# Recurrent branch's matmul units by token instead of by feature, its convolution spread over two units

## The reference

```python
h = rmsnorm(x, norm_mix_pre[l])
proj = h @ w_in[l]
xr, yr, q, k, v, g_rnn, g_attn = jnp.split(proj, IN_OFFSETS, axis=-1)
xr = causal_depthwise_conv(xr, conv_w[l], conv_b[l])   # y[s] = b + sum over k of xr[s-3+k] * w[k]
xr = rg_lru(xr, positions, ...)                        # gates by 256x256 blocks, then a scan over tokens
y_rnn = xr * jax.nn.gelu(yr)
q = rope(...); k = rope(...)
y_att = sliding_window_sink_attention(q, k, v, attn_sinks[l])
mix = sigmoid(g_rnn) * (y_rnn @ w_rnn_proj[l]) + sigmoid(g_attn) * (y_att @ w_attn_proj[l])
```

## Time and profile before

| | us |
|---|---|
| time, median of 3 runs | 2236.02 (2235.87 to 2236.43) |
| time of the profiled execution | 2235.79 |
| its span in the profile | 2234.1 |
| PE busy | 2226.4 (100%) |
| DVE busy | 1576.0 (71%) |
| ACT busy | 1223.8 (55%) |
| GpSimd busy | 274.0 (12%) |

### The profile page before, as it was taken

One profiled execution on the slowest core, in us unless ns is written; L12 is line 12 of the kernel. 1 busy time (PEld: TensorE's weight loads), 2 busy tenths in 40 slices (PEclk: granted clock), 3 DMA queues, 4 the chain that ended last, 5 costly groups with the idle time before them and its releaser, 6 DMA issues.

```text
span 2234.1 us, 32770 instructions
## 1 busy us (share of the span) xinstructions
PE 2226.4 (100%) x11630; PEld 1873.3 (84%) x11630; DVE 1576.0 (71%) x2081; ACT 1223.8 (55%) x1925; POOL 274.0 (12%) x317
## 2 busy tenths in 40 slices
PE   9999999999999999999999999999999999999999
PEld 7888999888888888888888888889977788778887
DVE  7666657665664778757857856966999967766774
ACT  6666677544444456555555656556444446554443
POOL 1232220000000102111212121120000001100000
PEclk9999999999999999999999999999999999999999
DMA  7555554666666866666666666665666665555665
GB/s 245 156 166 150 152 179 146 194 192 194 194 189 198 255 197 200 214 206 191 219 205 193 216 209 203 193 220 184 181 187 203 195 180 175 162 161 178 198 200 167
DMA packets 215349, 427.09 MB, mean 191 GB/s; under 512 B 14096, under 2 KB 14384, under 8 KB 214960
## 3 DMA queue, kind: packets, MB, share of 16 engines
q1 hardware_dynamic: 206960, 398.57, 57.4%
q0 software_dynamic: 8048, 26.62, 3.8%
q10 hardware_dynamic: 208, 0.07, 0.0%
HBM read 414.71 MB, written 10.49 MB: 190 GB/s over the span
## 4 chain that ended last, share of the span: by engine, by line
PE 92%; DVE 4%; ACT 3%; issue 1%; DMA 0%; POOL 0%; SPq 0%; ACTq 0%; POOLq 0%; DVEq 0%
PE acc L2054 25%; PE acc L2056 25%; PE acc L2055 25%; PE acc L2046 4%; PE acc L2048 3%; PE acc L2049 3%; DVE w_lo L1217 1%; PE sides L2274 1%; PE tps L2284 1%; PE sides L2147 1%; ACT w_hi L677 1%; PE tps L2165 1%; PE acc L1997 1%; PE tps L2158 0%; DVE stg L1241 0%
## 5 line engine op out<-in xcount | busy, mean ns | idle before, releaser
L1217 DVE TENSOR_TENSOR w_lo<-raw,w_hi 128x1024 fp32r<-128x1024 f32 x752 | 928.4, 1244 | 581.6 <-ACT w_hi L677 575.9
L677 ACT ACTIVATE w_hi<-raw 128x1024 fp32r<-128x1024 f32 x752 | 789.7, 1058 | 727.6 <-PE acc L2056 594.2
L2054 PE MATMUL acc<-w_hi,h_hi 128*128 128x512 f32 x1424 | 563.0, 395 | 0.3 <-DVE w_lo L1217 0.2
L2056 PE MATMUL acc<-w_hi,h_lo 128*128 128x512 f32 x1424 | 554.8, 390 | 0.0
L2055 PE MATMUL acc<-w_lo,h_hi 128*128 128x512 f32 x1424 | 554.5, 389 | 0.0
L2054 PEld LDWEIGHTS acc<-w_hi,h_hi 128*128 128x128 f32 x1424 | 267.3, 188 | 66.1 <-issue 11.4
L2056 PEld LDWEIGHTS acc<-w_hi,h_lo 128*128 128x128 f32 x1424 | 267.3, 188 | 56.7
L2055 PEld LDWEIGHTS acc<-w_lo,h_hi 128*128 128x128 f32 x1424 | 267.6, 188 | 52.8
L2054 PE MATMUL acc<-w_hi,slab_dg_r 128*128 128x512 f32 x756 | 294.2, 389 | 0.0
L2055 PE MATMUL acc<-w_lo,slab_dg_r 128*128 128x512 f32 x756 | 294.1, 389 | 0.0
L2056 PE MATMUL acc<-w_hi,slab_dg_r 128*128 128x512 f32 x756 | 294.1, 389 | 0.0
(11 more groups left out here) (407 smaller groups left out, 2356.8 us busy)
## 6 DMA issues: line engine op xcount, KB each, us to landing
raw<-in_w_in_dram SPq DMA_DIRECT2D x328, 512.0 KB, 4.0
raw<-in_w_mlp_up_dram SPq DMA_DIRECT2D x128, 512.0 KB, 4.2
raw<-in_w_mlp_down_dram SPq DMA_DIRECT2D x128, 512.0 KB, 4.2
raw<-in_w_out_dram SPq DMA_DIRECT2D x64, 512.0 KB, 4.6
raw<-in_w_rnn_proj_dram SPq DMA_DIRECT2D x32, 512.0 KB, 3.9
raw<-in_w_attn_proj_dram SPq DMA_DIRECT2D x32, 512.0 KB, 4.1
trig_scratch<-tmp POOLq DMA_DIRECT2D x32, 256.0 KB, 4.8
raw<-in_w_proj_ssm_dram SPq DMA_DIRECT2D x16, 512.0 KB, 3.8
```

The source lines that it names most:

```text
L677: nc.scalar.activation(w_hi[:, j % RING], raw[:, j % RING], ACT.Copy).then_inc(hi_ready, 1)
L1217: V.tensor_tensor(w_lo[:, j % RING], raw[:, j % RING], w_hi[:, j % RING].bitcast(F32), ALU.subtract)\
L2054: T.matmul(o, hi[:, k, c], wh, start=first, stop=False)
L2056: ins = T.matmul(o, lo[:, k, c], wh, start=False, stop=last)
```

## The change

The four xr units are made by token. When one is done, ACT copies the result to SBUF with `rstd` as a scale per partition (`xr_stage`, two instructions), and DVE turns it in 16 transposes of 32-row blocks (`xr_turn`, eight pieces of two) into `xr_c`; `xr_out` is gone. For c = 0 to 2 five pieces lie in steps 1, 1, 3, 3, 5 of the second unit and three in steps 2, 2, 4 of the next xr unit; for c = 3 all lie in yr0, in steps 1, 1, 3, 3, 4, 4, 5, 5. ACT's taps come one a step, for c = 0 to 2 in steps 5 and 7 of the next xr unit and in steps 2 and 4 of the unit after that; for c = 3 in steps 6, 6, 7, 7 of yr0. GpSimd adds the taps of c - 1 between the norms of c, and those of c = 3 last; `load_rg(0)` goes to after the sums of c = 2. `xr_c` and the staging get buffers of their own per c. The loops over c of ACT and DVE are written out.

```diff
@@ GpSimd
                     for c in range(NH):
                         normalise(None, c, 0)
                         normalise(None, c, 1)
+                        if c:
+                            conv_sum(c - 1, 2)
                         normalise(None, c, 2)
+                        if c:
+                            conv_sum(c - 1, 1)
                         normalise(None, c, 3)
-                        for k in (2, 1, 0):
-                            conv_sum(c, k)
-                        if c == 0:
-                            load_rg(0)
+                        if c:
+                            conv_sum(c - 1, 0)
+                    pool.wait_ge(tap_ready, 4 * (NH - 1))
+                    load_rg(0)
+                    for k in (2, 1, 0):
+                        conv_sum(NH - 1, k)
                     pool.wait_ge(conv_ready, NH + 1)
                     load_rg(1)
@@ places
-        TAPS_AT = [8, 10, 13, 13]
+        XR_TURN_AT = [1, 1, 3, 3, 5, S + 2, S + 2, S + 4]
+        TAPS_AT = [S + 5, S + 7, 2 * S + 2, 2 * S + 4]
+        LAST_TURN_AT = [1, 1, 3, 3, 4, 4, 5, 5]
+        LAST_TAPS_AT = [6, 6, 7, 7]
@@ ACT
+                def xr_stage():
+
+                    unit_over(None, 0, (U_QX + 1 + 2 * c) * S)
+                    if c == NH - 1:
+                        act.wait_ge(stg_ready, T_QX + c + 1)
+                    for t in range(TT):
+                        ins = nc.scalar.activation(xr_stage_of(c)[:, t, :], tok(acc[0])[:, t, :], ACT.Copy, scale=rstd[:, t:t + 1])
+                    ins.then_inc(acc_free[0], 1)
                 def conv_taps(k):
 
                     if k == 3:
-                        act.wait_ge(acc_free[0], lin(i, 1, c + 2))
-                        act.wait_ge(conv_ready, lin(i, 1, c + 1))
+                        act.wait_ge(xr_turned, c + 1)
+                        act.wait_ge(conv_ready, c + 1)
@@ ACT, gates
-                    act.wait_ge(conv_ready, NH + 1)
+                    act.wait_ge(conv_ready, NH)
@@ DVE
+            def turn_two(n, to, of):
+
+                for q in (2 * n, 2 * n + 1):
+                    a, b = divmod(q, 4)
+                    src = of[32 * a:32 * a + 32, :, :].rearrange("p t (m q i) -> p t m q i", q=4, i=32)[:, :, :, b, :]
+                    dst = to[32 * b:32 * b + 32, :, :].rearrange("p m (t q i) -> p t m q i", t=TT, q=4)[:, :, :, a, :]
+                    ins = V.transpose(dst, src)
+                return ins
+                def xr_turn(n):
+                    if n == 0:
+                        dve.wait_ge(acc_free[0], c + 2)
+                        if c == 2:
+                            dve.wait_ge(tap_ready, 4)
+                    ins = turn_two(n, xr_c[c], xr_stage_of(c))
+                    if n == 7:
+                        ins.then_inc(xr_turned, 1)
-            def xr_out(i, c):
-                unit_over(i, 2 * S, (U_QX + 1 + 2 * c) * S)
-                rows_ = row[:, :].unsqueeze(1).broadcast_to([P, QPC, SEQ])
-                dve.wait_ge(row_copied, 1)
-                dve.wait_ge(conv_ready, lin(i, 1, c + 1))
-                V.tensor_tensor(xr_c, feat(acc[0]), rows_, ALU.mult).then_inc(acc_free[0], 1)
@@ TensorE
-                unit(None, 0, u * S, 0, u, h_hi, h_lo, by_feature=True, hooks=beside_xr)
+                unit(None, 0, u * S, 0, u, h_hi, h_lo, hooks=beside_xr)
-            unit(None, 0, (U_QX + 2 * NH - 1) * S, 0, U_QX + 2 * NH - 1, h_hi, h_lo, by_feature=True, hooks=beside_xr)
+            unit(None, 0, (U_QX + 2 * NH - 1) * S, 0, U_QX + 2 * NH - 1, h_hi, h_lo, hooks=beside_xr)
```

More of the change, by code:

```diff
@@ L179, in griffin_block_then_ssm_block @@
         part_hi, part_lo = sem("part_hi"), sem("part_lo")
+        xr_turned = sem("xr_turned")
         side_landed = sem("side_landed")
@@ L358, in griffin_block_then_ssm_block @@
         xc4 = stg[:, :, :].rearrange("p t (k c) -> p (t k) c", c=SEQ)
-        xr_c = i4
+        xr_c = [slab_g[:, 0:4, :], i4, slab_g[:, 0:4, :], tmp2[:, :, :].rearrange("p t (k c) -> p (t k) c", c=SEQ)]
         yr_c = [k_t[:, :, :], xc4]
@@ L636, in griffin_block_then_ssm_block, with xr_stage_of @@
         TURN_P_AT = [13, 18, 23, 28]
-        TAPS_AT = [8, 10, 13, 13]
+        XR_TURN_AT = [1, 1, 3, 3, 5, S + 2, S + 2, S + 4]
+        TAPS_AT = [S + 5, S + 7, 2 * S + 2, 2 * S + 4]
+        LAST_TURN_AT = [1, 1, 3, 3, 4, 4, 5, 5]
+        LAST_TAPS_AT = [6, 6, 7, 7]
+        def xr_stage_of(c):
+            if c == NH - 1:
+                return tmp
+            return slab_d[:, (c + 1) * QPC:(c + 2) * QPC, :].rearrange("p k c -> p (k c)").rearrange("p (t n) -> p t n", t=TT)
         Y_ATT_AT = [(k + 3) // 2 for k in TURN_P_AT]
@@ L820, in conv_taps @@
                             ins = nc.scalar.activation(slab_d[:, span(i, QPC, QPC * c + m), :].rearrange("p o c -> p (o c)"),
-                                                       xr_c[:, m, :], ACT.Identity, scale=w, bias=b)
+                                                       xr_c[c][:, m, :], ACT.Identity, scale=w, bias=b)
                         else:
-                            ins = nc.scalar.activation(taps[k][:, m, 3 - k:], xr_c[:, m, 0:SEQ - 3 + k], ACT.Copy, scale=w)
+                            ins = nc.scalar.activation(taps[k][:, m, 3 - k:], xr_c[c][:, m, 0:SEQ - 3 + k], ACT.Copy, scale=w)
                     ins.then_inc(tap_ready, 1)
-                places = [(2, q_copy)]
+                places = [(2, q_copy), (S, xr_stage)]
                 for p, at in enumerate(SOFT_AT):
                     places += [(at + 1, lambda p=p: exps(p)), (Y_ATT_AT[p] - 1, lambda p=p: pt_copy(p)), (Y_ATT_AT[p], lambda p=p: y_hi(p))]
-                places += [(at, lambda k=k: conv_taps(k)) for at, k in zip(TAPS_AT, (3, 2, 1, 0))]
-                return placed(places, S, 2)[0]
+                if c == NH - 1:
+                    places += [(S + at, lambda k=k: conv_taps(k)) for at, k in zip(LAST_TAPS_AT, (3, 2, 1, 0))]
+                    return placed(places, S, 2)[0] + [[]]
+                return placed(places, S, 2)[0] + [[(at - S, lambda k=k: conv_taps(k)) for at, k in zip(TAPS_AT, (3, 2, 1, 0))]]
             def k_copy():
@@ L836, in _ @@
             steps(None, 0, U_QX * S, {3: [lambda: row_copy(1)], 4: [exponentials], 5: [k_copy]})
[L837 to L842, removed]
+            late = []
+            for c in range(NH):
+                beside_xr, beside_yr, next_late = attention(None, c)
+                for at, f in late:
+                    (beside_xr, beside_yr)[at // S].setdefault(at % S, []).append(f)
+                late = next_late
+                steps(None, 0, (U_QX + 1 + 2 * c) * S, beside_xr)
+                if c < NH - 1:
+                    steps(None, 0, (U_QX + 2 + 2 * c) * S, beside_yr)
             def y_high(c):
@@ L1236, in two @@
                         dve.wait_ge(sum_ready, lin(i, stride, index + 1))
[L1237 to L1241, removed]
+                    ins = turn_two(n, turned4, tmp)
                     if n == 7:
@@ L1413, in rotate_q @@
                 unit_over(i, 2 * S, (U_QX + 2 * c) * S)
-                if i is None:
+                if c == 0:
                     dve.wait_ge(tps_ready, T_K + 1)
@@ L1449, in attention @@
                     places += [(at, lambda p=p: soft(p)), (at + 2, lambda p=p: totals(p)), (Y_ATT_AT[p], lambda p=p: y_lo(p))]
-                return placed(places, S, 2)[0]
-            def xr_out(i, c):
-                unit_over(i, 2 * S, (U_QX + 1 + 2 * c) * S)
-                rows_ = row[:, :].unsqueeze(1).broadcast_to([P, QPC, SEQ])
-                dve.wait_ge(row_copied, 1)
-                dve.wait_ge(conv_ready, lin(i, 1, c + 1))
-                V.tensor_tensor(xr_c, feat(acc[0]), rows_, ALU.mult).then_inc(acc_free[0], 1)
+                turns = [lambda n=n: xr_turn(n) for n in range(8)]
+                places += [(S + at, f) for at, f in zip(LAST_TURN_AT if c == NH - 1 else XR_TURN_AT, turns) if at < S]
+                late = [(at - S, f) for at, f in zip(XR_TURN_AT, turns) if at >= S and c < NH - 1]
+                return placed(places, S, 2)[0] + [late]
             steps(None, 0, U_QX * S, {3: [lambdas], 5: [softplus]})
             rotate_q(None, 0)
[L1461 to L1470, removed]
+            late = []
+            for c in range(NH):
+                beside_xr, beside_yr, next_late = attention(None, c)
+                for at, f in late:
+                    beside_xr.setdefault(at, []).append(f)
+                late = next_late
+                steps(None, 0, (U_QX + 1 + 2 * c) * S, beside_xr)
+                if c < NH - 1:
+                    steps(None, 0, (U_QX + 2 + 2 * c) * S, beside_yr)
+                    rotate_q(None, c + 1)
             no_reset = keep[:, 0:1, :].broadcast_to([P, QPC, SEQ])
@@ L1518, in _ @@
                 unit_over(None, 0, u * S)
+                if c == 0:
+                    dve.wait_ge(row_copied, 1)
                 rows_ = row[:, :].unsqueeze(1).broadcast_to([P, QPC, SEQ])
```

## The result

| | us |
|---|---|
| before, median of 11 runs | 2236.13 |
| changed, median of 11 runs | 2241.53 (2240.97 to 2242.48) |
| ratio | 1.0025, 95% interval 1.0017 to 1.0032 |
| span of the profiled execution, before and changed | 2234.1 and 2240.2 |

The change makes the kernel slower by a quarter of a per cent, 5.4 us; 2234.2 was forecast, with 2239.0 as the end of the range.

What follows compares the result with a forecast made beforehand. PE's own work was taken to bound the kernel. Form -4.3, yr0 +2.1, q2 and q3 +0.4, first sum +0.1, xr0 +0.1 give -1.6 us from 2235.79, forecast 2234.2 us; range 2231.0 to 2239.0.

Steps and rivals of the forecast that it cites:

- the form: Four xr units by token, 96 matmuls of 512 columns for 192 of 256: 1.08 us less each, 4.3 us in all.
- What is hidden as a sum: Taps, staging copy and transposes on ACT and DVE stay under each unit's length and add nothing to PE's path.
- Rival D: Beside the attention the token form gains nothing and only the waits stay: 2238.5 us, chance 0.05.
- The port, its mechanism: GpSimd's sum and a DVE instruction with two SBUF inputs exclude each other; issue order decides which one waits.
- The walk of q2 and q3: Step 3's split held, four transposes, totals(3)'s reciprocal 1.2 us later: turn_p(3) stalls PE 0.2 us in each unit.
- The walk of yr0: Sums hold DVE's splits of steps 3 and 5, y_lo(2) comes late, and PE stalls 2.1 us before turn_p(3).
- wrong at its root: Sign of failure: an xr unit under 27 us, or stalls on another engine's chain, above all ACT's in yr0.
- The tenth of a microsecond: In yr0 GpSimd's third sum starts just ahead of DVE's step 5 split; if DVE came first, 2.1 us falls to nothing.
- rg(0): Gates' weights and y_lo(3), needed after yr0, have slack about equal to the stall: nothing added, 0 to 2 us in range.
- y_lo(0) and xr0: First sum delays y_lo(0) before turn_p(1) in three places, 0.1 us together; xr0's turn waits 0.1 us for rotate_q.
- Rival C: Sums of taps before norms hold splits with PE's pieces queued behind: +10.1 us, 2245.9 us, chance 0.14.
- six places: Stalls before turn_p(1) and turn_p(3) beside c = 1, 2 and 3, each at a full 2.4 us.

Runs made afterwards that it cites:

- e5: e2 with all four taps of c = 3 in step 7 of yr0, behind y_hi(3): 2231.86 us (ratio 0.9981).
- e4: The kernel before with only the four xr units made by token, its recurrent numbers not the reference's: 2233.17 us (ratio 0.9985).
- e1: The changed kernel with GpSimd's sum of the second tap waiting for soft(3)'s last instruction: 2235.6 us (ratio 0.9997).
- e3: The kernel before with one sum of taps moved between normalise(2) and normalise(3), nothing else: 2243.18 us (ratio 1.0032).
- e6: e5 with the second sum of taps back between normalise(2) and normalise(3): 2237.77 us (ratio 1.0008).
- e2: The changed kernel with each group's second and third sums after y_lo(2), behind normalise(3), and load_rg(0) before them: 2237.93 us (ratio 1.0009).
- e7: The changed kernel profiled once more, nothing altered: one execution, 2241.03 us.

## Why the prediction was wrong, point by point

**What bounds the kernel; the form.** Right. PE's sum of work set the time, and the xr unit fell to 27.30 us where 27.3 was forecast. The 4.3 us stand nearly whole in e5 (4.15 by the medians). In e4 0.4 us in each of three units went to ACT, a wait that the prediction didn't look for because it added up ACT's work by unit and never set PE's earlier arrival against it.

**What is hidden as a sum.** Right: with all transposes, the staging copy and all taps, e5's units have no gap but 0.15 us in xr0. Rival D is out.

**The port, its mechanism.** Right in kind: a sum of taps holds a DVE instruction with two SBUF inputs for its rest, and which is first decides. e1, e3 and e6 show it from three sides. In q2 of the changed kernel, though, the split's row starts 0.01 us ahead of the third sum's, and the sum still took its 2.35 us while the split took 3.43: at such a distance the rows don't tell who comes first.

**The walk of q2 and q3: the step that failed.** I wrote "split of step 3 held, four transposes" and a stall of 0.2 us each. The second sum starts where `normalise(2)` ends, and at that moment DVE is not at the split but still in `soft(3)`, two instructions before it. I put only splits, which are long, on the list of what can be held, and took it that `soft` runs free. The row that contradicts this stands in the trace of the kernel before, right ahead of the split in yr0 that I walked with the earlier trace rows; `normalise(2)` had ended 0.23 us before it began.

```profile
267.64 0.17 DVE L1433 SCALAR_TENSOR_TENSOR att<-att,pi 128x4 f32<-128x4 f32 x1
```

This instruction makes 512 numbers in all, both its inputs lie in SBUF, and the sum held it for 2.0 us in the changed kernel. And it is worth more than a split: a held split eats into a lead of three steps, while behind this one stand `exps(3)`, a split, `pt_copy(2)` and `by_v(2)`, with little slack. In e5, where it runs free, `pt_copy(2)` ends 0.27 us before `by_v(2)` begins in q2 and q3 and 0.77 us in yr0; where PE waits for it, 0.05 us. So 2.0 us of holding leave 1.8, 1.8 and 1.3 us of stall, which is what the changed kernel has. e3 prices it alone at 6.8 us for four places.

The rest of q2 and q3 is `turn_p(3)`, 1.5 us each (in the first profile hidden in q2 by the slower clock). I had `y_lo(2)` held in yr0 only; in q2 I set the split of step 5 beside `normalise(3)`, as it was before. In the changed kernel ACT's tap in step 4 (1.68 us) stands ahead of that step's split, and DVE's half of it begins at the very moment the third sum does (162.11 and 162.12 above). The third sum's part in this is shown by e6, where it waits for `y_lo(2)` and no gap stands before `turn_p(3)`. So the two terms of 0.2 us measured 3.3 and 3.2.

**The walk of yr0.** The sum was off by a little and its parts by more: 2.1 forecast, 2.6 measured, of which 1.3 is `turn_p(3)` behind the held split, by the way that was walked but not its 2.1, and 1.3 the `by_v(2)` that I had missed. That the total came near is luck. The prediction had named a stall on ACT's chain in yr0 as a sign of being wrong at its root, and this is one: `by_v(2)` waits for ACT, which waited for DVE, which the sum had held. The tenth of a microsecond fell as forecast, GpSimd first: its third sum started at 279.67 and the split at 279.77, which then took 3.36 us.

```profile
279.67 2.39 POOL L538 TENSOR_TENSOR slab_dg_f<-slab_dg_f,slab_i_f 128x1012 f32<-128x1012 f32 x1
...
279.77 3.36 DVE L1246 TENSOR_TENSOR w_lo<-raw,w_hi 128x1024 fp32r<-128x1024 f32 x1
```

**rg(0).** Put at nothing, measured 0.6 us. It was `y_lo(3)`, queued behind the taps of c = 3 by way of ACT, and not the gates' weights: it ended at 292.91 and `rg(0)` began at 293.05, and in e5, with the taps behind `y_hi(3)`, the gap is gone. The prediction listed that queue, put nothing for it into the sum and kept 0 to 2 us in the range; e2 shows that it can cost 4.1 us of waiting and 1.8 us of lower clock after it.

**y_lo(0) and xr0.** The first sum was expected to cost 0.1 us in three places together, and costs nothing. xr0's turn waited 1.0 us in the profiled execution, where a load of weights landed late and delayed a split, then `softplus` and `rotate_q`; in the other runs of kernels with the token form it is 0.2 or less, the forecast's size.

**The sum.** -4.3 + 3.3 + 3.2 + 2.6 + 0.6 + 0.2 = 5.6 us without the odd microsecond of xr0, against 5.4 by the medians. Rival C is what happened in kind: the port's mechanism, passing the bound. It had a chance of 0.14. Of its six places the three before `turn_p(3)` do wait, for 1.5, 1.5 and 1.3 us and not for 2.4 each; the three before `turn_p(1)` don't; and the larger part, three waits before `by_v(2)`, was not on its list. The range was too narrow because each stall's upper end was given to a place in the text (0 to 1.5, 0 to 2, 2.4) and then not added: together they reach beyond 2241 us.

## What to carry to other kernels

When an instruction of GpSimd is moved, list every DVE instruction with two SBUF inputs that may fall into its time, the smallest ones too, and price each by the chain that hangs on it and not by its own length. Put long GpSimd work behind the last short piece that a chain needs, by a wait on that piece's semaphore: e1's one line was worth 5.9 us, more than the form's whole gain. And when work is moved later to be out of the way, ask first who waits for it; in e2 the answer cost 5.8 us and in e5 a change of two numbers in a table gave it back.

## What was not expected of the hardware

A wait of PE can cost more than its length. In e2 the wait before `rg(0)` was 4.1 us and the time lost 5.8. In the first profile of the changed kernel the gap before `by_v(2)` in q2 was followed by matmuls that start 0.43 us apart and not 0.227, for 3.5 us:

```profile
160.88 0.63 PE L2096 MATMUL acc<-w_lo,h_hi 128*128 128x512 f32 x1
161.31 0.63 PE L2097 MATMUL acc<-w_hi,h_lo 128*128 128x512 f32 x1
161.74 0.63 PE L2095 MATMUL acc<-w_hi,h_hi 128*128 128x512 f32 x1
```

The busy time by stretches of the same kernel, with the granted clock after the engines, shows a mean of 0.57 from 160 to 164 us and 1.00 around it: the lower of the two levels, 1.2 GHz, for most of the stretch.

```profile
157.00:160.00 3.00, 1.27 (x12) 0.78 (x12) 2.65 (x5) 3.00 (x9) 0.00 (x0) 1.00 0.52 170
160.00:164.00 4.00, 4.00 (x19) 3.05 (x16) 2.25 (x4) 2.35 (x5) 3.46 (x3) 0.57 0.44 137
164.00:168.00 4.00, 4.00 (x23) 3.35 (x21) 3.94 (x5) 1.88 (x2) 0.46 (x1) 1.00 0.27 54
```

From the first matmul behind `by_v(2)` to the ninth after it took 164.15 - 160.40 = 3.75 us; in e7, at the full clock, the same took 161.76 - 159.58 = 2.18 us. So the dip cost 1.6 us, after a stretch in which PE was busy for 1.27 of 3 us. It did not lengthen q2, because `y_lo(2)` would have been late anyway.

The same gap in q3, in e7's q2 and q3, in e3's four units and in e6 was followed by no dip in the profiled executions. But the mean granted clock of every execution is on record, and it goes with the gaps. That mean is 1.0 in all 49 executions of the kernel before in the two comparisons, and in all of e1's 10, e4's 10 and e5's 11. It is 0.999 in 8 of 11 of the changed kernel, in 6 of 10 of e6 and in 2 of 7 of e3, which have the gap before `by_v(2)`, and 0.998 or 0.999 in all 10 of e2, which has the gap before `rg(0)`. In e6 and e3 the executions at 0.999 are the longest, in e3 2244.4 us against 2242.3 to 2243.4; in the changed kernel, where a late `y_lo(2)` follows, they are not. So the dip does not come with every gap, but it comes with the programs that have these gaps.
